# A hybrid recurrent/pooling encoder layer on one core: down products of both output halves side by side, banks taken by age, operand buffers that change roles

## The reference

```python
proj = rmsnorm(x) @ w_in                       # 1024 -> 4096: x_A | x_B | g_A | g_B
y_a = rg_lru(causal_conv4(x_A))                # two 128x128 gate products per head, then a scan
y_b = pool_mix(x_B)                            # means over 2, 4, 8, 16 frames, minus x_B
merged = sigmoid(g_A) * (y_a @ w_br_a) + sigmoid(g_B) * (y_b @ w_br_b)
x = x + merged @ w_out
g, u = split(rmsnorm(x) @ w_gu)                # 1024 -> 2 * 2816
x = x + (silu(g) * u) @ w_down                 # 2816 -> 1024
y = rmsnorm(x)
```

## Time and profile before

| | us |
|---|---|
| median of 3 runs | 2899.11 (2894.8 to 2900.23) |
| the profiled execution | 2899.26 |
| its span, first to last instruction | 2897.4 |
| PE busy / DVE busy / ACT busy | 2720.9 / 2104.6 / 1367.3 |
| mean granted clock of PE | 0.981 of full |

### The profile page before, as it was taken

How to read it: one execution, slowest core, us unless ns; L and a number is a source line. 1 busy time by engine, 2 the same in 40 slices (tenths; PEclk the granted TensorE clock), 3 DMA queues, 4 the chain that set the end, 5 groups by cost and what they waited for, 6 DMA issues and landing times.

```text
span 2897.4 us, 39533 instructions
## 1 busy us (share of the span) xinstructions
PE 2720.9 (94%) x15404; PEld 2676.2 (92%) x15404; DVE 2104.6 (73%) x2784; ACT 1367.3 (47%) x1849; POOL 250.6 (9%) x425
## 2 busy tenths in 40 slices
PE   8999999999999999999799999889999979999995
PEld 6999999999999999999799999789999979899995
DVE  6867788688868877876676566787666677666667
ACT  6743583366447544833444343454344435334442
POOL 2000101020110011021300000300000030000000
PEclk9999999999999999999899999999999999999998
DMA  6353567456655855574543443445343434534442
GB/s 225 125 180 122 187 224 265 150 202 240 212 184 184 280 190 174 201 260 139 178 154 131 133 128 127 130 142 197 125 131 131 133 129 143 190 124 131 131 131 87
DMA packets 166729, 481.87 MB, mean 166 GB/s; under 512 B 18800, under 2 KB 41840, under 8 KB 166544
## 3 DMA queue, kind: packets, MB, share of 16 engines
q1 hardware_dynamic: 124368, 345.21, 35.7%
q0 software_dynamic: 31664, 117.66, 11.8%
q10 hardware_dynamic: 10512, 16.46, 2.0%
HBM read 414.75 MB, written 64.51 MB: 165 GB/s over the span
## 4 chain that ended last, share of the span: by engine, by line
PE 67%; DVE 15%; ACT 7%; issue 5%; DMA 2%; POOL 2%; SPq 0%; DVEq 0%; ACTq 0%; POOLq 0%
PE ps L635 67%; DVE wring L1590 2%; ACT wring L795 2%; DVE xacc L1579 1%; DMA work<-ys 1%; DVE tmp L1336 1%; DVE work L1545 1%; DVE gb L1305 1%; DVE tmp L1439 1%; POOL work L557 1%; ACT work L1056 1%; DVE main L1721 1%; DVE tmp L1252 1%; DVE xlo L1256 1%; ACT L896 1%
## 5 line engine op out<-in xcount | busy, mean ns | idle before, releaser
L1590 DVE TENSOR_TENSOR wring<-wraw,wring 128x1024 fp32r<-128x1024 f32 (+1 forms) x637 | 768.1, 1206 | 298.8 <-ACT wring L795 296.6
L795 ACT ACTIVATE wring<-wraw 128x1024 fp32r<-128x1024 f32 (+1 forms) x637 | 661.6, 1039 | 620.1 <-PE ps L635 616.6
L635 PE MATMUL ps<-ycomb,wring 128*128 128x346 f32 (+1 forms) x5544 | 890.7, 322 | 23.3 <-issue 14.0
L635 PEld LDWEIGHTS ps<-ycomb,wring 128*128 128x128 f32 x5544 | 887.3, 190 | 25.0 <-issue 25.0
L635 PE MATMUL ps<-xhi,wring 128*128 128x416 f32 (+1 forms) x2560 | 707.7, 354 | 32.9 <-DVE wring L1590 27.6
L635 PE MATMUL ps<-hcomb,wring 128*128 128x346 f32 (+1 forms) x2772 | 477.2, 333 | 90.9 <-DVE xacc L1579 65.8
L635 PEld LDWEIGHTS ps<-hcomb,wring 128*128 128x128 f32 x2772 | 461.3, 197 | 104.8 <-issue 82.4
L635 PEld LDWEIGHTS ps<-xhi,wring 128*128 128x128 f32 x2560 | 482.3, 188 | 47.3 <-DVE wring L1590 26.4
L635 PE MATMUL ps<-xlo,wring 128*128 128x416 f32 (+1 forms) x1280 | 451.5, 353 | 0.0
L635 PE MATMUL ps<-yhi,wring 128*128 128x416 f32 x1280 | 347.1, 351 | 2.6 <-DVE wring L1590 2.6
L1579 DVE TENSOR_TENSOR xacc<-ps,xacc 128x692 f32<-128x692 f32 (+1 forms) x252 | 218.3, 877 | 94.4 <-PE ps L635 90.8
(11 more groups left out here) (209 smaller groups left out, 2231.7 us busy)
## 6 DMA issues: line engine op xcount, KB each, us to landing
wraw<-dwm SPq DMA_DIRECT2D x247, 512.0 KB, 3.5
wraw<-sgu SPq DMA_DIRECT2D x132, 512.0 KB, 3.2
wraw<-graw SPq DMA_DIRECT2D x99, 512.0 KB, 3.4
wraw<-sdn SPq DMA_DIRECT2D x120, 256.0 KB, 2.8
wraw<-draw SPq DMA_DIRECT2D x90, 256.0 KB, 2.9
pbuf<-graw POOLq DMA_DIRECT2D x22, 1024.0 KB, 6.9
sgu<-pbuf POOLq DMA_DIRECT2D x22, 1024.0 KB, 6.2
wraw<-fused SPq DMA_DIRECT2D x40, 512.0 KB, 3.3
```

What stands on the lines that cost most here:

```text
L635: mm = nc.tensor.matmul(out, wt[:, c * P:(c + 1) * P], x, start=(first and q == 0), stop=(last and q == 2), skip_group_check=chain)
L795: A(wring[:, n % RING, 0, 0:c], wraw[:, n % RAW, 0:c], ACT.Copy, scale=cst[:, PSC, name[2]:name[2] + 1] if name[0] == "w" else 1.0).then_i ...
L1590: V.tensor_tensor(wring[:, n % RING, 1, 0:c], wraw[:, n % RAW, 0:c], wring[:, n % RING, 0, 0:c].bitcast(f32), SUB).then_inc(w_lo, 1)
```

## The change

- Five down groups in place of six; the last one holds pairs 8, 9 and 10. Its first three half-steps issue the matmuls of pairs 8 and 9 before they wait for pair 10, and those of pair 10 afterwards.
- In `down`, the two output halves of one product follow each other (k outer, `mp` inner). Every product takes its bank pair from a list of the pairs by age of last use: role 0 takes the oldest pair for `mp` = 0 and the second oldest for `mp` = 1, the other roles the third and fourth oldest.
- A down weight tile is loaded with one DMA of 1024 columns; in the group of three pairs each half-step has its own tile of 768 columns.
- `x` and `y` buffers change roles from block to block, and in blocks 0 to 3 the merged branches are written into the block's `x` buffer. `mhi`/`mlo` serve the last block alone; in part of their place lies a fourth entry of `wring` (`wextra`), used up to the last block's `b` products.
- The 33 chunks of `prepare` go on through the `b` steps (`PREPARE`), and the load of chunk i + 2 is issued right behind the store of chunk i.
- Operand loads are issued one step ahead of their use (`operand_in`); those of the first pass start before the first `o` step. `BUILD`, `TAKE` and `REBUILD` are set anew.
- In the last pass all eight `norm_square` come after the last down product. In the group before, three of them stood among the down steps.

```diff
-GROUPS = ((0, 1), (2, 3), (4, 5), (6, 7), (8, 9), (10,))
-NCH = 2 * PAIRS + 2 * len(GROUPS)
+GROUPS = ((0, 1), (2, 3), (4, 5), (6, 7), (8, 9, 10))
+NCH = 3 * PAIRS
...
-    r = (r + 1) // 2 % 4
+    age = [(r // 2 + q) % 4 for q in range(4)]
...
         cleared[pair] += reads
+        age.remove(pair)
+        age.append(pair)
...
-            for mp in range(2 if what == "dn" else 1):
-                for k, prod in enumerate(PROD):
-                    hold([(what, s, i, mp, k, v) for v in range(2)], (r + ROLE[prod]) % 4, 2 if (what, prod) == ("gu", 4) else 1)
-                r = (r + 3) % 4
+            pairs = tuple(age)
+            for k, prod in enumerate(PROD):
+                if what == "gu":
+                    hold([("gu", s, i, 0, k, v) for v in range(2)], pairs[ROLE[prod]], 2 if prod == 4 else 1)
+                    continue
+                for mp in range(2):
+                    hold([("dn", s, i, mp, k, v) for v in range(2)], pairs[mp + (2 if ROLE[prod] else 0)], 1)
...
-BUILD = {0: 0, 2: 1, 4: 2, 5: 3}
-TAKE = {2: 0, 4: 1, 6: 2, 7: 3}
-REBUILD = {2: 0, 3: 1, 5: 2, 6: 3}
+BUILD = {1: 1, 3: 2, 5: 3}
+TAKE = {0: 0, 2: 1, 4: 2, 6: 3}
+REBUILD = {3: 0, 6: 1, 9: 2, 12: 3}
...
+PLACE = [n % (RING if n >= NARROW else RING + 1) for n in range(NS)]
...
+        def x_of(b):
+            return opnd[b % 2]
+        def y_of(b):
+            return opnd[1 - b % 2]
+        def merged_of(b):
+            return x_of(b) if b < NB - 1 else (mhi, mlo)
...
+                steps = [(k, mp) for k in range(7) for mp in range(2)]
+                if width == 3:
+                    pe.wait_ge(h_hi, 4 * n - 4)
+                    pe.wait_ge(h_lo, 4 * n - 4)
+                    for k, mp in steps[:3]:
+                        hold(("dn", s, g, mp, k, 0))
+                        part(k, mp, (0, 1))
                 pe.wait_ge(h_hi, 4 * n)
                 pe.wait_ge(h_lo, 4 * n)
...
+                for i, (k, mp) in enumerate(steps):
+                    if width == 3 and i < 3:
+                        part(k, mp, (2,))
+                    else:
+                        hold(("dn", s, g, mp, k, 0))
+                        part(k, mp, tuple(range(width)))
...
+                for i in chunks[late:]:
+                    prep_store(i)
                 if b == NB - 1:
                     pool.wait_ge(merged, NB * KT)
                     pool.wait_ge(y_kept, 16 * KT * 2)
+                    operand_in(0, 0)
+                    operand_in(0, 1)
+                    operand(0, 0)
...
-                act.wait_ge(*clear(dn(s, len(GROUPS) - 1, m % 4 // 2, 6)))
+                act.wait_ge(*clear(dn(s, LASTG, 1, 6)))
```

More of the change, by code:

```diff
@@ L154, in slot_order @@
         for what, i in STEPS:
-            out += [(what, s, i, k) for k in range(7)]
+            out += [(what, s, i, k) for k in range(dn_units(i) if what == "dn" else 7)]
     return out
@@ L184, in slot_width, with splits_after @@
     name = SLOTS[n]
[L185 to L194, removed]
+    return 768 if name[0] == "dn" and dn_units(name[2]) == 14 else KT * P
+LANDED = [16 * (n // RAW + 1) for n in range(NS)]
+NARROW = SLOT[("b", NB - 1, 0)]
+PLACE = [n % (RING if n >= NARROW else RING + 1) for n in range(NS)]
+PREV = [max([m for m in range(max(0, n - 9), n) if PLACE[m] == PLACE[n]], default=-1) for n in range(NS)]
+RELEASE = list(itertools.accumulate(PREV, max))
+def splits_after(k):
+    return [n for n in range(k + 1, min(k + 6, NS)) if RELEASE[n] == k]
 def side_unit(b, p):
@@ L363, in prep_ends, with prep_index, ring @@
                 half = slice(512 * v, 512 * v + 512)
[L364 to L371, removed]
+                return graw[p, :, :, half], sgu[p, :, :, half]
+            cols = slice(512 * (i - 2 * PAIRS), 512 * (i - 2 * PAIRS) + 512)
+            return draw[:, :, cols], sdn[:, :, cols]
+        def prep_index(b, what, i):
+            n = PREPARE[b].index((what, i)) if b and (what, i) in PREPARE[b] else len(prep_range(b))
+            return list(prep_range(b))[n:n + 1]
+        def ring(n):
+            return wring[:, PLACE[n]] if PLACE[n] < RING else wextra[:]
+        def x_of(b):
[4 more added lines that the diff above has]
+            return x_of(b) if b < NB - 1 else (mhi, mlo)
         def sum_before(kind, b):
@@ L418, in raw @@
                     _, _, g, j = name
[L419 to L423, removed]
+                    k, first = (j, 0) if dn_units(g) == 7 else (j // 2, 768 * (j % 2))
+                    c = GCOL[g] + first
+                    src, q = (draw, PLAIN[PROD[k]]) if PROD[k] in PLAIN else (sdn, SUMMED[PROD[k]])
+                    sp.dma_start(slot[:, 0:slot_width(n)], src[q, :, c:c + slot_width(n)]).then_inc(raw_in[n % RAW], 16)
                 elif name[0] == "b":
@@ L615, in weights @@
                 pe.wait_ge(w_lo, n + 1)
-                return wring[:, n % RING, 0, :], wring[:, n % RING, 1, :]
+                return ring(n)[:, 0, :], ring(n)[:, 1, :]
             def side(v):
@@ L692, in down, with part @@
                 n, width = s * PAIRS + GROUPS[g][-1] + 1, len(GROUPS[g])
+                def part(k, mp, terms):
+                    wh, wl = weights(SLOT[("dn", s, g, k if width == 2 else 2 * k + mp)])
+                    c, first = COMBO[PROD[k]], 4 * mp if width == 2 else 0
+                    for v in range(2):
+                        out = bank(("dn", s, g, mp, k, v))[:, 0:TH[s]]
+                        for t in terms:
+                            z = GROUPS[g][t] % 3
+                            mm = product(out, wh, wl, first + width * v + t, hcomb[:, z, 0, c, 0:TH[s]], hcomb[:, z, 1, c, 0:TH[s]],
+                                         t == 0 and PROD[k] in OPENS, t == width - 1 and PROD[k] in ENDS, True)
+                        if terms[-1] == width - 1:
+                            mm.then_inc(ready, 1)
@@ L730, in _ @@
                 for h in range(KT):
-                    full(("xa", b, h), xhi, xlo, {k: ((xn_hi, n8 + k + 1), (xn_lo, n8 + k + 1)) for k in range(KT)} if h == 0 else ())
+                    full(("xa", b, h), x_of(b), {k: ((xn_hi, n8 + k + 1), (xn_lo, n8 + k + 1)) for k in range(KT)} if h == 0 else ())
                     if h == 2 and b == 0:
@@ L957, in quad @@
                     act.wait_ge(scanned, h + 1)
-                    A(yhi[:, h, 0:W], part(j, 0), ACT.Copy).then_inc(ya_hi, 1)
+                    A(y_of(0)[0][:, h, 0:W], part(j, 0), ACT.Copy).then_inc(ya_hi, 1)
                     if j == 0:
```

265 lines of the change are left out of this document (132 added, 133 removed).

## The result

The changed kernel takes 2776.31 us (median of 4 runs, 2775.59 to 2778.35) against 2899.4 for the kernel before (the three runs of the table above and a fourth), a ratio of 0.958 with a 95% interval of 0.9563 to 0.9596. The forecast was 2769, with a range from 2742 to 2812. The profiled execution has a span of 2775.1 us, 122.3 less.

The account below looks back on a forecast made before the run. PE, busy 94% of the span, was taken as the bound, with only its waits and lower-clock time to win. Savings of 57.5 + 35.4 + 9.4 + 13.1 + 15 = 130.4 us take 2899.3 to 2769, range 2742 to 2812.

Parts of the forecast that it names:

- A: Down groups 0 to 3, twelve times: two bank-pair stalls shrink to one of 0.55 us, saving 57.5 us.
- the second rival: The clock keeps dropping behind the 0.55 us stalls that stay: 2791 us, chance 0.12.
- B: End of the passes: last group takes 47.7 us in passes 0 and 1, 41.8 in pass 2; saves 35.4 us.
- The first rival: At the end of passes 0 and 1, GpSimd's differences hold DVE for their full length: 2801 us, chance 0.11.
- C: Between mixer and feed-forward part: earlier operand loads leave 2.5 us idle before the first gate-up, saving 9.4 us.
- D: Behind a pass's first pair: the norm's column sum and the gate-up get different old bank pairs, saving 13.1 us.
- E: Mixer: a fourth ring entry puts weight splits further ahead of PE, winning 15 of 21.5 us of waits.
- The third rival: Mixer gets slower: `prepare` in the `b` steps pushes the merge back, losing 8 us: 2792 us, chance 0.09.

Follow-up runs that it names:

- The experiment with loads in halves: Changed kernel, with the next pass's first four tiles loaded after only their own four stores, the other four afterwards: 2766.00 us.
- the run with age alone: Kernel before, with bank pairs taken from the list by age and the old order of output halves: 2898.81 us.
- The run with GpSimd on 8 columns: Changed kernel, with GpSimd's three differences for operands of passes 1 and 2 made on 8 columns in place of 346: 2767.45 us.
- the rotating counter: Changed kernel, with bank pairs taken from a rotating counter in place of the list by age: 2798.79 us.

## Why the prediction was right, and where its terms were off

**A was right in mechanism and nearly in size.** An ordinary group stands for 0.26 to 0.34 us where I had 0.55, and takes 27.3 us where I had 27.35. The two groups that wait for `xacc` were sized too low: they came to 3.5 and 5.8 us over an ordinary one, against the 0.3 and 4.6 I left them. In pass 1 that load had been nearly hidden by the two stalls, so taking them away laid it bare. The experiment with loads in halves took both away, 9.4 us in its profile. I had taken the new order of the halves and the age list together; the runs part them. In these groups the order does 43.8 of the 54.0 us, the age list the other 10.2, and the age list with the old order makes them 8.9 us longer. (The upper bound that I gave for A should be 64: 57.5 and twelve times 0.55.)

**The clock came along.** I took the drops to the lower level to go with the stalls. Ten groups with about 0.3 us of idle time all show 1.00, which answers the second rival. The converse showed in the run with age alone, where one stall of 4.2 us was followed by a lower clock in all twelve groups.

**B came out within 2.8 us, but partly by luck.** The group takes 48.3 and 48.0 us where I had 46, the half-clocked matmuls behind pass 0 are there and those behind pass 1 are not. The tail grew by 1.9 us, not 2.6. The way to the 46 us was wrong in two places. I had 41.4 us of work for DVE and some 5 us in which it waits for GpSimd's differences; it has 45.7 us of work and does not wait for them. And I had PE wait 1.5 us for pair 10 and 3 us for the last operand; it waits 3.9 us for splits, none of it for pair 10, and 2.0 us for the operand. The errors nearly cancel.

The first rival, that GpSimd and VectorE exclude each other, is true as a mechanism and small as a price. Where a difference of GpSimd and an instruction of DVE met, the timeline of the changed kernel shows DVE's instruction longer, in this case by the full length of the former:

```profile
1375.10 2.41 DVE L1296 TENSOR_TENSOR tot<-tot,sq 128x416 f32<-128x416 f32 x1 [0.62 <-ACT sq L883]
1375.35 1.70 POOL L594 TENSOR_TENSOR work<-work 128x696 f32<-128x696 f32 x1
```

and the same line without such a neighbour:

```profile
1380.50 0.59 DVE L1296 TENSOR_TENSOR tot<-tot,sq 128x416 f32<-128x416 f32 x1 [0.61 <-ACT sq L883]
```

That is 1.82 us longer for a neighbour of 1.70. The Trainium skill's rule (SBUF — State Buffer, section "SBUF: two separate sides"), that the shared port is an exclusive lock for a whole instruction, agrees with it in length. By the recorded starts DVE's instruction began 0.25 us before GpSimd's and was still the one held, so the rows do not show which of two meeting instructions has to wait; starts on GpSimd are rough. My reading of 0.7 to 0.8 us for each meeting was too mild: in the last group of pass 0 five of DVE's instructions are longer, by 0.7 to 2.1 us (two splits take 3.07 and 3.09 us where the others take 0.95). But they come to some 6 us, not the 18 that I gave the rival, which had every difference hold DVE for its full length: the adds of line 1637 keep their 0.87 us beside GpSimd. The run with GpSimd on 8 columns wins 6.1 us of DVE's time, and 4.2 of the group.

**C is the step that failed in size.** It won 3.7 us where I had 9.4. I let the last operand be ready 2.5 us behind the mixer's last matmul, which gave 2.5 us of idle time. It was ready 5.4 us behind it, and the idle time was 7.25. Three things were missed. First, the initial order of the age list gives the first gate-up the bank pair of the mixer's last product, so it waits for an add that stands behind the last operand's low parts in DVE's queue; that changed the releaser and 1.6 us of idle time when it was mended, with no sure change in the median. Second, the last operand waits for its `o` step on ACT: GpSimd's first difference is done at 1377.05, and ACT takes it up at 1380.37, behind the square of that step. One step earlier took 3.0 us of idle time away. Third, that square waits for an add on DVE which stands behind two instructions made longer beside GpSimd: the 2.41 us above for 0.59, and a split of 1.95 us for 1.22. That is 2.5 us on the chain, read from the trace; no run takes it away for pass 0. The three stalls of about 1 us inside `o` were as forecast (1.05, 1.47 and 1.44).

**D was right** (14.4 for 13.1), and the rotating counter shows its reason: its three waits of 3.17 and 2.89 us came back with it.

**E was right in sum, by a route I had only half.** The fourth entry takes away all 16.9 us of waits for splits behind the first 100 us (the 4.0 in `o` belong to C), and waits in the first 100 us are 2.9 us less: 19.8 of my 21.5, where I took 15. For the chunks in the `b` steps I had DVE's idle time as a cover, and looked for the price at the first `o` product. It is paid at the normed input of the next block instead: PE's waits for it are 8.0 us in place of 5.2, and moving two chunks back brings them to 4.5 and wins 5.2 us. The third rival named this mechanism; the fourth entry outweighed it. (The 17.4 us in the table compare one execution of each kernel, and the end of the mixer moves by 3 us from one execution to the next.)

Of the forecast of what the profile would show, one point was clearly missed: less than 5 us idle before the first gate-up (7.25). Three more were near or in part: the group of three pairs at 48.3 and 48.0 us for 46 to 48, at 42.9 in pass 2 for near 42, and ten of the twelve groups at 27 to 28 us and full clock, not the two that wait for `xacc`.

## What to carry to other kernels

When an accumulator is needed again before its reader's queue gets to it, look for independent work to put between, and then choose which buffer each piece takes; here the order of the work gave most of the gain in the groups, and the choice of the buffer gave nothing without it. Ask of every stall taken away what was hidden beneath it: in pass 1 the load for the next pass cost 0.4 us beside two stalls of 4 us together, and 3.5 us without them. Ask of a wait for several transfers whether the first piece of work needs all of them: one wait for eight stores held back loads that needed only four of them. An operation tied by hand to a step of another loop is worth one run with the tie one step earlier.

## What the hardware showed beyond that

- In these groups, idle time of 0.3 us was never followed by a lower clock. Two stalls of about 1.6 and 2.35 us, with 12 matmuls between them, were in nine of twelve cases (in two of the nine the second was longer, 2.79 and 5.26 us), and one stretch of 4.2 us in eleven of eleven, at about the same total. The length alone does not tell: 2.50 us in the changed kernel was followed by a lower clock (20.79 us for 120 matmuls), 3.18 us in the run with GpSimd on 8 columns was not (19.34).
- A VectorE instruction with two operands in SBUF was longer by the length of a GpSimd instruction beside it: 2.41 us for 0.59 beside one of 1.70. One with an operand in PSUM was not: line 1637 took 0.87 us at 1806.85, inside a GpSimd instruction that ran from 1806.19 to 1807.72.
